# Down-projection weights of the experts issued by ScalarE on its own DMA queue, gate and up weights left on SyncE's

## The reference

```python
def hier_moe(h, w_rg, b_rg, w_re, b_re, w_eg, w_eu, w_ed):
    t = h.reshape(b * s, d)                       # 576 rows x 1024
    ...                                           # top-1 of 4 groups, then top-2 of 8 experts, weights in comb
    for g in range(N_EXPERT_GROUPS):
        a = jnp.einsum('nd,edf->nef', t, w_eg[g]) # gate, 1024 -> 256
        u = jnp.einsum('nd,edf->nef', t, w_eu[g]) # up,   1024 -> 256
        act = jax.nn.silu(a) * u * comb[:, g, :, None].astype(t.dtype)
        out = out + jnp.einsum('nef,efd->nd', act, w_ed[g])   # down, 256 -> 1024
```

## Time and profile before

| | us |
|---|---|
| median of 3 runs | 1204.61 |
| lowest and highest of the runs | 1200.33 and 1204.88 |
| span of the profiled execution | 1184.3 |
| what the median has beside this span | 20.3 |

### The profile page before, as it was taken

The page is one execution under the profiler, slowest core; times in us unless marked ns, Lnnn a source line. Parts: engine busy times, 40 slices in busy tenths (PEclk is TensorE's granted clock), DMA queues, the critical chain, the costliest instruction groups (busy, mean ns, idle before and its releaser), DMA issues. The chain is left out here.

```text
span 1184.3 us, 19295 instructions
## 1 busy us (share of the span) xinstructions
PE 1046.9 (88%) x7440; PEld 641.5 (54%) x7440; DVE 333.7 (28%) x881; ACT 261.0 (22%) x585; POOL 243.6 (21%) x257
## 2 busy tenths in 40 slices
PE   3999999997998699799998999999968998787870
PEld 2444444444565477577776766764545554444430
DVE  3100033226862432122232210232451231000105
ACT  3000000013553132223232221312222111111114
POOL 1000043301200100455403565000013332212110
PEclk9999999999998699899999999999978998889895
DMA  9976666877877889999999986877088999999966
GB/s 330 372 281 251 251 251 251 314 231 248 261 248 248 265 242 292 364 325 353 327 340 342 353 270 205 302 274 310 36 347 290 367 380 384 380 391 380 408 243 239
DMA packets 120726, 353.69 MB, mean 299 GB/s; under 512 B 15578, under 2 KB 59362, under 8 KB 109886
## 3 DMA queue, kind: packets, MB, share of 16 engines
q1 hardware_dynamic: 91166, 289.37, 68.1%
q0 software_dynamic: 16576, 46.42, 11.5%
q10 hardware_dynamic: 12896, 16.69, 4.3%
HBM read 336.38 MB, written 67.55 MB: 341 GB/s over the span
## 5 line engine op out<-in xcount | busy, mean ns | idle before, releaser
L1364 POOL DMA_INDIRECT w_all<-in_cache_b_v,value_rows x128 | 121.1, 946 | 213.7 <-PE bank L1482 128.8
L422 PE MATMUL bank<-w_all,turned 128*128 128x481 f32 (+2 forms) x384 | 119.3, 503 | 1.1 <-DVE turned L640 1.1
L422 PE MATMUL bank<-w_ring,turned 128*128 128x481 f32 (+2 forms) x384 | 118.7, 502 | 0.0
L1391 PE MATMUL bank<-ident,w_all 128*128 128x128 f32 x720 | 100.1, 292 | 19.2 <-DMA w_all<-in_cache_b_k 9.1
L1885 PE MATMUL bank<-w_all,mix_row 128*64 128x256 f32 x736 | 94.6, 415 | 24.8 <-DMA w_all<-in_w_exp 23.7
L1391 PEld LDWEIGHTS bank<-ident,w_all 128*128 128x128 f32 x720 | 85.0, 149 | 33.9 <-DMA w_all<-in_cache_b_k 11.5
L1885 PEld LDWEIGHTS bank<-w_all,mix_row 128*64 128x64 f32 x736 | 62.2, 150 | 63.9 <-issue 44.5
L1629 DVE COPY mods<-bank 128x512 f32<-128x512 f32 x90 | 62.1, 691 | 106.8 <-PE bank L1391 103.0
L422 PEld LDWEIGHTS bank<-w_all,turned 128*128 128x128 f32 (+1 forms) x384 | 56.8, 171 | 61.5 <-issue 58.4
L422 PEld LDWEIGHTS bank<-w_ring,turned 128*128 128x128 f32 (+1 forms) x384 | 57.1, 171 | 60.1 <-issue 56.9
L1566 ACT ACTIVATE mods<-bank 128x512 f32<-128x512 f32 x90 | 53.1, 596 | 100.3 <-PE bank L1391 100.3
(11 more groups left out here) (337 smaller groups left out, 1309.4 us busy)
## 6 DMA issues: line engine op xcount, KB each, us to landing
w_all<-in_w_exp SPq DMA_DIRECT2D x22, 2048.0 KB, 40.4
w_all<-in_cache_b_k SPq DMA_DIRECT2D x128, 256.0 KB
out_a_sample<-in_cache_a SPq DMA_DIRECT2D x8, 4080.0 KB, 20.9
w_all<-in_w_exp SPq DMA_DIRECT2D x25, 1024.0 KB, 38.5
w_all<-in_cache_a SPq DMA_DIRECT2D x96, 256.0 KB, 7.6
mods<-in_w_ada SPq DMA_DIRECT2D x21, 1024.0 KB, 8.1
turned<-in_w_exp SPq DMA_DIRECT2D x5, 2048.0 KB, 42.2
mods<-in_w_exp SPq DMA_DIRECT2D x5, 2048.0 KB
```

The costliest lines, as they stand in the source:

```text
L422: mm = nc.tensor.matmul(m.banks[i][r:r + ROWS[i], 0:hi - lo], m.hT[:, k, i * P:i * P + ROWS[i]], ring[u][:, CW * k + lo:CW * k + hi], star ...
L1364: pool.indirect_dma_start(out=vr[k % RINGS][2 * j + y], out_offset=None, in_=value_rows, in_offset=bass.IndirectOffsetOnAxis(ap=v_row[:, p ...
L1391: mm = nc.tensor.transpose(T(b)[:, y * P:(y + 1) * P], buf[part][:, c:c + P], m.ident[:, :])
```

## The change

SyncE no longer issues the down weights of blocks 6 to 31, and no longer waits for the down matmuls before them. ScalarE issues them instead: after the copy of the result of block n (`result_out`), it issues the down weights of block n + 6, on its own DMA queue, where n + 6 is below 32. The condition under which the slot is free is the same, since `result_out` has waited for the down matmuls of block n. Gate/up of all blocks, and both parts of block 32, whose expert is known only at run time, stay with SyncE.

```diff
@@ SyncE, the loop over b in range(RING, EXPERTS) and what follows
                 sp.wait_ge(S["gu"], b - RING + 1)
                 weights_in(I["w_exp"][b], b, GATE_UP, m.w_in[b % RING])
-                if b > RING:
-                    sp.wait_ge(S["down"], b - RING)
-                    weights_in(I["w_exp"][b - 1], b - 1, DOWN, m.down_in[(b - 1) % RING])
             sp.wait_ge(own_ok, 1)
             first = owner(slice(0, 1))
             sp.wait_ge(S["gu"], EXPERTS - RING + 1)
             weights_in(first, EXPERTS, GATE_UP, m.w_in[EXPERTS % RING])
-            sp.wait_ge(S["down"], EXPERTS - RING)
-            weights_in(I["w_exp"][EXPERTS - 1], EXPERTS - 1, DOWN, m.down_in[(EXPERTS - 1) % RING])
             sp.wait_ge(S["down"], EXPERTS - RING + 1)
             weights_in(first, EXPERTS, DOWN, m.down_in[EXPERTS % RING])
@@ ScalarE, step(t, before, third)
                 if third:
                     result_out(S, act, third)
+                    b = third.n + RING
+                    if b < EXPERTS:
+                        act.dma_start(m.weights(b)[:, DOWN], I["w_exp"][b][:, DOWN]).then_inc(m.down_in[b % RING], 16)
```

## The result

The changed kernel takes 1223.9 us (median of 4 runs, 1218.3 to 1226.5) against 1202.5 for the kernel before on the same chip: a ratio of 1.0187, with a 95% interval of 1.0148 to 1.0225. It is slower by 21.5 us. The forecast was +1.3 us and the range ended at 1218.

A forecast was written before the change was run, and what follows sets the result against it. The prediction took bytes through full DMA engines as the bound, with PE waiting for weights. Its terms were 0 us except +1.3 us for order, giving span 1185.6 plus 20.3 us unchanged, 1205.9 us, range 1195 to 1218.

The forecast's parts named there:

- What bounds the kernel: Expert stage: from 981.30 us on, bytes are the bound at 388 GB/s, PE waits for them, 8.94 us a block.
- Bytes, issue by ScalarE, SyncE: Expert stage: same 55 loads, ScalarE's 26 issues hidden in its idle time, SyncE on no path; 0 us each.
- Later release: Down loads stand behind ScalarE's copy, 0.60 us later, but the engines don't run dry: 0 us, at most 0.6 once.
- Order: End of the stage: two queues take turns, so gate/up 32 lands 1.3 us later: +1.3 us.
- Rate, with two queues full: Expert stage: large packets from both hardware queues keep the full DMA rate, 0 us; +7 us if 3% were lost.
- The wait for the gathers: Expert stage, only a sign of being right: gathers land later than 8.9 us but PE doesn't wait for them.
- the gather phase stretches: Rival, expert stage: gather phases of lower DMA rate last 1.7 times as long, +15.7 us, time 1221.6; chance 0.14.
- Blocked ScalarE: Rival: ScalarE stands at its load issues, 3.8 us hidden, at 9.4 us each +23 us, time 1229; chance 0.03.
- SyncE as the bound: Rival: SyncE's issue bounds the stage and half its issues leave it, at most -17 us, time 1188; chance 0.02.
- The signs to look for: Right: 26 ScalarE loads, short issues, 388 GB/s, gate/up 32 within 2 us of 1142. Wrong: rate under 375 or over 400.
- The 20.3 us beside the span: Whole kernel: the profiled span of 1184.3 us is 20.3 below the median 1204.6; taken as unchanged.

The follow-up runs named there:

- behind_copy: Kernel before, one queue, but SyncE's down weights of blocks 6 to 31 wait for ScalarE's copy instead of the down matmuls: ratio 1.0030 to the kernel before.
- swapped: Changed kernel with the queues exchanged: ScalarE issues gate/up of blocks 7 to 31 behind its Silu, SyncE all down weights: ratio 1.0167 to the kernel before.
- gate_up_halves_one_queue: Kernel before, all loads on SyncE's queue, gate/up of blocks 7 to 31 cut into two loads with 8 KB rows: ratio 0.9981 to the kernel before.
- same_kernel: The kernel before with no edit, as a control beside itself: ratio 0.9996.
- both_halves: Changed kernel, two queues, with gate/up cut into loads with 8 KB rows and down into 4 KB rows: ratio 1.0022 to the kernel before.
- gate_up_halves: Changed kernel, two queues, with only gate/up of blocks 7 to 31 cut into two loads with 8 KB rows: ratio 1.0061 to the kernel before.

## Why the prediction was wrong, point by point

- *What bounds the kernel* (bytes, at 388 GB/s): right, and it still holds for the bytes. The rate stayed at 385. A full set of DMA engines alone wasn't the whole bound: PE needs rows as well as weights, and the rows come through the same engines by turns.
- *Bytes, issue by ScalarE, SyncE*, 0 us each: right. ScalarE's 26 issues took 334 ns at the median, 350 at most, SyncE's went back from 3773 to 328, and behind_copy and swapped leave no room for the release or the place.
  In the changed kernel's trace (ns min/median/max):

```profile
L1965 SPq DMA_DIRECT2D w_all<-in_w_exp x21: 327/328/357, 914.3 to 1153.5; - x21
```

```profile
L2303 ACTq DMA_DIRECT2D w_all<-in_w_exp x18: 334/334/350, 924.3 to 1146.2; - x18
```

- *Later release*, 0 us: right by its price (behind_copy), wrong in its reason. It said that nothing is lost through the wait on the scatter, issued 25 us earlier. The scatters landed 35.1 us after their issue at the median, and ScalarE waited 61.7 us for them.

- *Order*: packets do take turns one to one; that row was read rightly. The +1.3 us at the end never came to bear, since PE was no longer waiting for gate/up.
- *Rate, with two queues full*, 0 us: right as a rate, 385 against 388 GB/s.
- *The wait for the gathers* is the step that failed. The sum has no term for it, and the prediction gives no reason; it says only, among the signs, that the gathers land later but PE doesn't wait for them. The runs showed landings after 33 to 39 us instead of 8.9, and 42.7 us of waits of PE beyond the first. Of the gathers I asked only what they cost in rate.
- *The rival "the gather phase stretches"*, 1221.6 us, came within 2.3 us of the result for a wrong reason. That is luck: it priced a loss of rate of 15.7 us, and there is none, though a gather is always in the queue (one is issued every 10 us and lands after 33 to 39). Its quote of the Trainium skill ("DMA: Bandwidth & Descriptors", "Queues, rings and completion order") has an engine drain a packet of some 9 to 17 descriptors before it goes on. The trace agrees with going round the queues and differs on the turn: the profile has a record for each row, and such records alternate singly at 95% of the steps. The equal counts alone would not tell the two apart, the order does.
- *Blocked ScalarE*, *SyncE as the bound*: both refuted by the 334 ns, and by gate_up_halves_one_queue, in which SyncE issues more loads at no cost.
- *The signs to look for*: ScalarE's 26 loads, the issues of both engines, the share and the rate came out as given under "right", and none of the signs under "wrong" came. Two signs under "right" failed: "PE doesn't wait for them", with 47.9 us, and the start of gate/up 32, 278.0 us after the first gather (1183.01) instead of 255.7. The only cover that I had worked out was four blocks, 25 us at PE's pace, for the scatter, and I didn't ask what fills a queue that is served more slowly than it is fed.
- *The 20.3 us beside the span* were added as unchanged. The changed kernel's profiled execution took 1226.5 us with a span of 1224.7, so 1.8 us lie outside the span. The other 18.5 are the difference of 18.6 us ahead of the stage: as it seems, the profile of before was taken on another chip than its times. The forecast isn't hurt, since it adds the change to the time of before.

How 22.0 us come about: counted from the first gather, the turn of block 29 comes at 255.0 us (1160.06) in the changed kernel, and it is the last that waits. What is left is 31.6 us of nearly pure PE work, some five steps of 6.22 us, whatever the weights do. In before, with weights as the bound, the last gate/up starts at 255.7 us (1142.14) and only 8.9 us are left after it. The stage ends 22 us later for that.

## What to carry to other kernels

Before loads are moved to a second hardware queue, or cut into larger rows, count packets, not bytes, on every queue that shares the DMA engines: the packets that each needs for a step of the loop against the turns it gets. Count the slots of a gather or scatter, as it seems even the empty ones (below). A queue of many small packets (a gather, a scatter) lives on the turns that the packets of the others give it. Where both hardware queues are wanted, cut the rows of the large loads until the small queue has turns to spare, and keep the shares of bytes in the ratio in which they are used.

## What the runs showed of the hardware that I had not expected

- Turns go by packet, whatever its size. Packets of 16 KB, of 8 KB and the small ones of a gather were moved in counts equal within 1% (2432, 2431 and 2450), and in the order of one each. With 24 KB rows on one queue they were equal within 3% (2471 and 2531).
- A packet of 4 bytes takes a turn like one of 16 KB, though it keeps its engine for 9 ns at the median against 630 (changed kernel, 960 to 1110 us).
- Empty slots seem to cost turns. Of the 5280 packets of GpSimd's queue, 2292 have 4 KB, 24 have about 2 KB, 2016 have 4 bytes and 948 have 8. The 33 blocks have 64 slots each, 2112 in all, of which the experts' 1152 rows leave 960 empty. 1152 rows gathered and 1152 scattered (as two half rows in a packet), 960 empty slots on each side and 16 completions for each of the 66 transfers make 5280. That the small packets are the empty slots is read from this sum; no run has changed the number of empty slots.
- A queue near its bound is already late: a need of 112 with 144 turns, and of 160 with 216, gave landings of 22 and 23 us at most. A need of 160 with 288 gave 9.4 to 10.1 at most (before, same_kernel, behind_copy, both_halves), but 16.3 in gate_up_halves with 292, for which no run shows the cause.
- The same code took some 18 us more ahead of the expert stage in some profiles than in others. The first gather stands at 884 to 890 us in that of before and in those of two chips, at 902 to 905 in that of the changed kernel and in those of a third chip. The stage of the changed kernel differed by 2.8 us between the two kinds (286.6 and 283.8). Each chip of the experiments was used in one batch only, so chip and batch can't be told apart.
